# A decoder trunk on one core: norm and router as one stage, the shared expert moved ahead of the routed pairs

## The chip, the cores and the metric

The kernel runs on one core of one Trainium2 chip. The metric is the device time of one execution in microseconds (us), lower is better. All data is float32.

## What is computed

The input is a sequence of 272 tokens (16 learned meta tokens and 256 given ones) of width 1024. Two residual layers follow. Layer 0 mixes tokens with a gated linear recurrence and a gated delta rule side by side, layer 1 with a state space model and a gated output projection. Each mixer, and each mixture of experts (MoE) behind it, is closed by a LayerNorm over the sum of the scaled input and the result. Cut to the lines that the change touches:

```python
for layer in range(DEPTH):                       # DEPTH = 2
    mix = _ab_mixer(h, ...) if layer % 2 == 0 else _s5_mixer(h, ...)
    h = _layer_norm(ALPHA * h + mix, ln_mix_g[layer], ln_mix_b[layer])
    ffn = _moe_ffn(h, ...)
    h = _layer_norm(ALPHA * h + ffn, ln_ffn_g[layer], ln_ffn_b[layer])

def _moe_ffn(h, ...):
    scores = sigmoid(h @ w_router)                # 64 experts
    biased = scores + router_bias
    # 8 groups of 8 experts; a group's score is the sum of its two best; 4 groups stay
    # the 8 best biased experts of those groups are chosen; their scores, made to sum to 2.5, are the gates
    routed = sum over chosen e of gate_e * (silu(h @ w_gate[e]) * (h @ w_up[e])) @ w_down[e]   # 1024 -> 256 -> 1024
    shared = (silu(h @ sh_gate) * (h @ sh_up)) @ sh_down
    return routed + shared
```

Layer 1 computes its MoE for the 256 given tokens only (W = 256, two token tiles); layer 0 for all 272 (W = 272, three token tiles, the last of 16 tokens).

## The kernel before, in words

The activations `hT` lie in SBUF with the channels on the 128 partitions: 8 channel tiles (DC = 8) of W tokens each. Every stage is a block of its own with one hand-written program per engine: PE (matmuls), ACT (activations, copies), DVE (elementwise), POOL and SP (which issues most DMAs). The order of the work on an engine is the order in which it is written, and semaphores order the engines against each other. At the end of a block all engines meet before the next block begins.

For each layer the stages around the change are these.

- **The end of the mixer.** In layer 0 `group_mixers` projects to 8 output tiles; PE's L703 does the matmuls of a tile, DVE's L1035 adds it to `hT`. In layer 1 the gated projection (L2270 on PE, L2283 on ACT, L2289 and L2291 on DVE) does the same.
- **`layer_norm` (L1111 on).** PE sums over channels by multiplying with a matrix of ones (L1145, 8 matmuls), DVE makes the mean (L1174) and subtracts it from each tile (L1177), ACT squares each (L1160), PE sums the squares (L1149), ACT takes the root (L1162), DVE the reciprocal (L1179), DVE multiplies each tile (L1182), ACT applies gain and shift (L1166). For layer 0 SP issues, at the start of this stage, the router's weights and tables (L1089 to L1092), the shared expert's weights (L1095, L1097) and the weights of the first two pairs of experts (L1076, L1082). The norm behind the MoE (`source="acc"`) first adds `acc` to `hT` on DVE (L1172); the last one is the last stage but the writing out. In layer 0 that norm's block also carries SP's loads for the next mixer (L2059 to L2071).
- **`router_and_shared` (L1187 on).** PE makes the logits with `hT` as the stationary operand and the router's weights moving (L1228, 3 x 8 matmuls of 64 columns in layer 0), turns the normed tokens into rows (L1237), which ACT copies (L1275) and SP stores to DRAM (L1221), and multiplies with the shared expert's gate weights (L1243, 16 matmuls; ACT applies SiLU, L1278). DVE chooses the experts in a chain of small operations (L1293 to L1325), each of which waits for the one before. PE then makes the rank of each token within its expert (L1249) and turns mask and gates (L1255); DVE writes `places_gates` and the largest count (L1327 to L1336).
- **`experts` (L1339 on).** The 64 experts go in 32 pairs, 64 slots each. At the start three pairs are prepared one behind the other: DVE makes a selection (L1588), PE spreads the pair's row of places and gates (L1438, L1439), ACT copies the gates (L1549), DVE makes the scatter matrix and the token indices (L1602, L1606, L1611), POOL gathers the tokens' rows (L1411). Then, per pair: gate and up projection (L1461), turning the next pair's tokens (L1447), turning the activation (L1482), the combine of the pair before into 8 tiles (L1474 on PE, L1629 on DVE into `acc`), the spreading for the pair three ahead, the down projection (L1494). ACT's SiLU (L1562) comes right behind the gate and up projection. SP loads the weights of pair q+2 into the place of pair q as its matmuls end. Behind pair 0 comes the shared expert's up projection (L1522, 16 matmuls) with DVE's product (L1658); behind each of pairs 1 to 4 come two of the 8 tiles of its down projection (L1531) and DVE's `hT = ALPHA * hT + ...` (L1664). Pairs 5 to 28 run in a hardware loop, four to an iteration, pairs 29 to 31 behind it.

## Time and profile before

| quantity | value |
|---|---|
| median of 3 runs | 1783.89 us |
| lowest and highest run | 1783.6 and 1790.15 us |
| the profiled execution's own time | 1779.24 us |
| its span in the profile | 1777.5 us |
| PE, busy share of the span | 92% |
| DVE, ACT, POOL, busy share | 43%, 21%, 14% |
| mean granted clock of PE | 0.952 |
| DMA, mean over the span | 295 GB/s |

The profile is of one execution. Busy time of PE is the time in which it has matmuls under way; the granted clock is the share of full speed at which PE may run, so the same matmul is longer at a lower one. A float32 matmul shows as two records, so 16 records are 8 matmuls; a turning (a transpose) shows as one.

### The profile page before, as it was taken

The numbers are of one execution on the slowest core, as the hardware profiler recorded it, in microseconds if no ns is written. First come the engines' busy times: TensorE is split into PE (matmuls) and PEld (weight loads), VectorE is DVE, ScalarE is ACT, GpSimd is POOL, SyncE is SP. The second block draws the span as 40 slices with busy tenths as digits, with TensorE's granted clock in tenths as the row PEclk, the third lists the DMA queues.
The fourth block names the chain that finished last, engine by engine and source line by source line (L and its number), as shares of the span: only waits on it lengthen the run. The fifth ranks groups of instructions, "written<-read, shape, count | busy, mean of one in ns | idle before, by whom it ended". The sixth has DMA issues, their size and how long they took to land. (4 is left out here: it accounts for less than half of the span.)

```text
span 1777.5 us, 26595 instructions
## 1 busy us (share of the span) xinstructions
PE 1633.7 (92%) x9863; PEld 987.4 (56%) x9863; DVE 769.3 (43%) x1814; ACT 380.3 (21%) x798; POOL 249.7 (14%) x325
## 2 busy tenths in 40 slices
PE   7999889897799999999999877977999999999995
PEld 5787668775345444444444456863544444444444
DVE  3879567413234344334433455132434433443334
ACT  3765452203001111111111110130111111111112
POOL 5789243000000000000000000000000000000000
PEclk9999998798899999999999968988999999999998
DMA  7688260028588999999999270664999999999970
GB/s 259 209 164 260 84 182 3 1 95 314 233 344 340 409 421 425 423 417 421 421 420 421 100 301 3 242 248 190 362 369 413 425 424 425 427 424 425 424 322 25
DMA packets 101518, 524.87 MB, mean 295 GB/s; under 512 B 34020, under 2 KB 39012, under 8 KB 66620
## 3 DMA queue, kind: packets, MB, share of 16 engines
q1 hardware_dynamic: 90780, 480.62, 68.4%
q0 software_dynamic: 10656, 43.13, 6.3%
q8 instruction: 56, 0.92, 0.2%
q14 instruction: 26, 0.21, 0.0%
HBM read 510.80 MB, written 17.10 MB: 297 GB/s over the span
## 5 line engine op out<-in xcount | busy, mean ns | idle before, releaser
L1461 PE MATMUL e_b<-experts,e_xgT 128*64 128x512 f32 x2048 | 454.9, 597 | 8.1 <-DVE hT L1664 5.2
L1461 PEld LDWEIGHTS e_b<-experts,e_xgT 128*64 128x64 f32 x2048 | 150.3, 138 | 298.1 <-issue 292.5
L1474 PE MATMUL e_b<-e_sg,e_ys 128*128 128x272 f32 (+1 forms) x1024 | 239.0, 386 | 1.7 <-ACT e_ys L1572 1.7
L1494 PE MATMUL e_b<-experts,e_aT 128*64 128x512 f32 x1024 | 233.9, 598 | 3.7 <-DVE acc L1629 3.7
L1635 DVE TENSOR_TENSOR e_ac<-e_sl,e_b 128x256 f32<-128x256 f32 x64 | 27.0, 422 | 441.3 <-ACT e_sl L1562 441.3
L1629 DVE TENSOR_TENSOR acc<-acc,e_b 128x272 f32<-128x272 f32 (+1 forms) x512 | 200.4, 427 | 17.1 <-PE e_b L1474 10.8
L1474 PEld LDWEIGHTS e_b<-e_sg,e_ys 128*128 128x128 f32 x1024 | 188.3, 190 | 33.8 <-ACT e_ys L1572 3.4
L1411 POOL DMA_INDIRECT e_xg<-rows_dram,e_idx x64 | 60.1, 939 | 980.3 <-DVE e_idx L1611 972.0
L241 PE MATMUL proj<-hT,dense_ring 128*128 128x272 f32 x768 | 185.8, 401 | 10.2 <-DMA dense_ring<-in_w_in 10.2
L241 PEld LDWEIGHTS proj<-hT,dense_ring 128*128 128x128 f32 x768 | 148.1, 194 | 44.1 <-issue 13.4
L1494 PEld LDWEIGHTS e_b<-experts,e_aT 128*64 128x64 f32 x1024 | 70.7, 136 | 133.3 <-issue 116.7
L1562 ACT ACTIVATE e_sl<-e_b 128x256 f32<-128x256 f32 x64 | 24.6, 384 | 448.2 <-PE e_b L1461 448.2
L1645 DVE COPY e_ys<-e_b 128x512 f32<-128x512 f32 x64 | 44.3, 692 | 136.9 <-PE e_b L1494 136.9
L1447 PEld LDWEIGHTS e_b<-ident,e_xg 128*128 128x128 f32 x512 | 56.2, 144 | 54.8 <-issue 52.5
L1572 ACT COPY e_ys<-e_b 128x512 f32<-128x512 f32 x64 | 37.5, 585 | 229.3 <-PE e_b L1494 229.3
L1549 ACT COPY e_gsb<-e_b 128x272 f32<-128x272 f32 (+1 forms) x64 | 24.2, 379 | 236.4 <-PE e_b L1439 236.4
L1447 PE MATMUL e_b<-ident,e_xg 128*128 128x128 f32 x512 | 71.6, 284 | 3.0 <-DVE e_hit L1606 3.0
L703 PE MATMUL mix<-y,dense_ring 128*128 128x272 f32 x256 | 60.9, 398 | 1.4 <-DVE y L1024 1.1
L411 DVE SCALAR_TENSOR_TENSOR qkv<-cin,conv_w,qkv 128x272 f32<-128x272 f32 x48 | 41.7, 870 | 42.6 <-ACT qkv L299 41.7
L1438 PE MATMUL e_b<-places_gates,e_selw 64*128 64x272 f32 (+1 forms) x128 | 48.0, 456 | 12.8 <-DVE e_selw L1588 12.8
L2270 PE MATMUL glu<-acc,dense_ring 128*128 128x256 f32 x256 | 58.3, 392 | 1.3 <-PEq L106 1.3
L703 PEld LDWEIGHTS mix<-y,dense_ring 128*128 128x128 f32 x256 | 49.0, 193 | 11.9 <-DVE y L1024 1.3
(389 smaller groups left out, 1743.4 us busy)
## 6 DMA issues: line engine op xcount, KB each, us to landing
experts<-in_moe_gate_up SPq DMA_DIRECT2D x128, 2048.0 KB, 12.3
experts<-in_moe_down SPq DMA_DIRECT2D x128, 1024.0 KB, 10.6
dense_ring<-in_w_in SPq DMA_DIRECT2D x48, 512.0 KB, 4.5
dense_ring<-in_w_out SPq DMA_DIRECT2D x4, 2048.0 KB, 7.9
dense_ring<-in_s_w_out SPq DMA_DIRECT2D x4, 2048.0 KB, 12.8
s_cw_dram<-s_out POOLq DMA_DIRECT2D x4, 1024.0 KB, 5.4
s_cw<-s_cw_dram SPq DMA_DIRECT2D x4, 1024.0 KB, 12.0
s_wb<-s_wb_dram SPq DMA_DIRECT2D x2, 2048.0 KB, 19.1
```

What stands on the lines that cost most here:

```text
L241: mm = pe.matmul(ps[g % 4][:, 0:T], slot[:, n % SLOTS_IN, c, :], hT[:, c, :], start=(c == 0), stop=(c == DC - 1))
L411: step.done(dve.scalar_tensor_tensor(out=dst, in0=src[:, j:j + T], scalar=w(j), in1=dst, op0=ALU.mult, op1=ALU.add))
L703: mm = pe.matmul(out, ring[:, m // 4, c, (m % 4) * P:(m % 4 + 1) * P], y[:, q * DC + c, :], start=(c == 0), stop=(c == DC - 1))
L1411: pool.indirect_dma_start(out=xg[:, u % 2, :], out_offset=None, in_=mem["rows_dram"], in_offset=bass.IndirectOffsetOnAxis(ap=idx[:, u, :], ...
L1438: pe.matmul(t0b[:, 0:W], selw[0:E, u % 2, :], pg[0:E, 0:W], start=True, stop=True)
L1447: mm = pe.transpose((t0b, t1b)[c // 4][:, (c % 4) * P:(c % 4 + 1) * P], xg[:, u % 2, c * P:(c + 1) * P], ident[:])
L1461: mm = pe.matmul(gub[e * SLOTS:(e + 1) * SLOTS, :], xgT[:, u % 2, c, e * SLOTS:(e + 1) * SLOTS], gu_w(2 * (u % 2) + e)[:, c, :], start=(c ...
L1474: pe.matmul(cb[m % 4][:, 0:W], ys[:, m * P:(m + 1) * P], sg[:, u, :], start=True, stop=True).then_inc(cmm, 1)
L1494: mm = pe.matmul(yb[e * SLOTS:(e + 1) * SLOTS, :], aT[:, f, e * SLOTS:(e + 1) * SLOTS], dn_w(2 * (u % 2) + e)[:, f, h * BLOCK:(h + 1) * BL ...
L1629: dve.tensor_tensor(acc[:, m, 0:W], acc[:, m, 0:W], cb[m % 4][:, 0:W], ALU.add).then_inc(addd, 1)
L1645: dve.tensor_copy(ys[:, BLOCK:], y1b[:]).then_inc(ye1, 1)
L2270: mm = pe.matmul(ps[m % 4][:, 0:W], ring[:, b % 2, c, (m % 4) * P:(m % 4 + 1) * P], yT[:, c, :], start=(c == 0), stop=(c == DC - 1))
```

## The change

1. The column sums of the norm behind the mixer go into the mixer's last stage, each behind the projection two tiles later.
2. That norm and the router become one stage, `norm_and_route`. The logits are taken from the centred, not yet scaled tiles with the router's weights (multiplied by the norm's gain, on POOL) as the stationary operand: 8 matmuls of W columns; scale and shift are applied to the 64 x W result, and the scores are turned to tokens-on-partitions. Root and reciprocal become Ln and Exp. Group comparison and top-8 are joined over the token tiles. The shared expert's up projection and product now stand in this stage.
3. For layer 0 all these loads are issued in this stage: router, shared expert, pair 0, then the rows' stores, then pair 1. For layer 1 the router's loads move ahead into the mixer's last stage.
4. In `experts` the three first pairs are spread into three different pairs of PSUM banks one right behind the other, and all 8 tiles of the shared down projection, with `acc = ALPHA * hT + ...`, stand ahead of pair 0. `acc` is no longer set to zero, the loop holds pairs 1 to 28, and the norm behind the MoE reads `acc` directly, without the addition.
5. PSUM is one tensor for the whole kernel instead of one set per stage.

```diff
@@ group_mixers, PE: column sums joined
+                def column_sum(m):
+                    pe.wait_ge(added, DC + m + 1)
+                    pe.matmul(bank[4][:, 0:T], mem["ones"][:], hT[:, m, :], start=(m == 0), stop=(m == DC - 1))
+
                 for m in range(DC):
                     project(m, 1)
+                    if m >= 2:
+                        column_sum(m - 2)
+                column_sum(DC - 2)
+                column_sum(DC - 1)
...
@@ layer_norm (the one behind the MoE)
-                    if source == "acc":
-                        pe.wait_ge(added, c + 1)
-                    mm = pe.matmul(sums[:, 0:W], ones[:], hN[:, c, :], start=(c == 0), stop=(c == DC - 1))
+                    mm = pe.matmul(sums[:, 0:W], ones[:], acc[:, c, 0:W], start=(c == 0), stop=(c == DC - 1))
...
-                act.activation(rstd[:], sqs[:, 0:W], ACT.Sqrt, scale=1.0 / D, bias=eps[:, 2:3]).then_inc(rooted, 1)
+                act.activation(rstd[:], sqs[:, 0:W], ACT.Ln, scale=1.0 / D, bias=eps[:, 2:3]).then_inc(logged, 1)
+                act.wait_ge(logged, 1)
+                act.activation(rstd[:], rstd[:], ACT.Exp, scale=-0.5).then_inc(rooted, 1)
...
-                dve.reciprocal(rstd[:], rstd[:]).then_inc(inverted, 1)
-                dve.wait_ge(inverted, 1)
...
@@ norm_and_route, SP
+                if layer == 0:
+                    load_router(sp, k, mem, 0)
+                load_shared(sp, k, mem, layer)
+                if layer == 0:
+                    load_gate_up(sp, k, mem, 0, 0, 0)
+                    load_down(sp, k, mem, 0, 0, 0)
                 for tt, (t0, n) in enumerate(tiles):
                     sp.wait_ge(rows_c, 2 * tt + 2)
                     sp.dma_start(mem["rows_dram"][t0:t0 + n, :], rows[0:n, tt, :]).then_inc(stored, 16)
+                if layer == 0:
+                    load_gate_up(sp, k, mem, 0, 1, 1)
+                    load_down(sp, k, mem, 0, 1, 1)
...
@@ norm_and_route, PE, behind the sums of squares
+                for c in range(DC):
+                    mm = pe.matmul(bias_ps[0:E, 0:1], wr[:, c, :], shift(c), start=(c == 0), stop=(c == DC - 1))
+                mm.then_inc(biased, 1)
+                pe.wait_ge(weighed, 1)
+                for c in range(DC):
+                    mm = pe.matmul(lg_ps[0:E, 0:W], wg[:, c, :], hN[:, c, :], start=(c == 0), stop=(c == DC - 1))
+                mm.then_inc(logits, 1)
+
+                pe.wait_ge(scored, 1)
                 for tt, (t0, n) in enumerate(tiles):
...
+                    mm = pe.transpose(sc_ps[0:n, tt * E:(tt + 1) * E], lgT[:, t0:t0 + n], ident[0:E, 0:E])
+                mm.then_inc(score_turned, 1)
+
                 for i in range(2 * NT):
                     tt, half = i // 2, i % 2
                     t0, n = tiles[tt]
+                    pe.wait_ge(out, 4 * half + 4)
...
+                shared_half(0)
+                shared_half(1)
                 pe.wait_ge(selected, 1)
...
                 pe.wait_ge(gated, 1)
...
+                shared_half(2)
+                shared_half(3)
                 pe.wait_ge(counted, 1)
...
@@ experts, PE
-                turn(0, 0, (AHEAD, 16))
+                pe.wait_ge(mem["shared_down_ready"], 16 * (layer + 1))
+                for m in range(DC):
+                    if m >= 2:
+                        pe.wait_ge(sh_out, m - 1)
+                    for c in range(FC):
+                        mm = pe.matmul(cb[m % 2][:, 0:W], sh_down_w[:, c, m * P:(m + 1) * P], shared_act[:, c, :],
+                                       start=(c == 0), stop=(c == FC - 1))
+                    mm.then_inc(sh_dn, 1)
+                turn(0, 0, (1, 16))
+                pe.wait_ge(idf_ok, AHEAD)
                 pair(0, 0, 0)
...
-                with pe.Fori(0, (FULL - SHARED) // 4) as i:
+                pe.wait_ge(sh_out, DC)
+                with pe.Fori(0, FULL // 4) as i:
...
@@ experts, DVE
                 for q in range(AHEAD):
-                    select(q, q)
-                    places(q, q)
+                    select(q, q, start=True)
+                places(0, 0)
+                places(1, 1)
+                for m in range(4):
+                    residual(m)
+                places(2, 2)
+                for m in range(4, DC):
+                    residual(m)
                 turned_in(0, 0, True)
                 pair(0, 0, early=True)
...
```

`shared_half(0)` and `(1)` are the 16 gate matmuls (into banks 3 and 7), `(2)` and `(3)` the 16 up matmuls. The copies of the mask and of the gates for `places_gates` go from DVE to ACT, behind its two SiLUs.

## Rows read from the trace of the kernel before

**Rows 1.** Stretches: length, busy time (instructions) per engine, granted PE clock, DMA share, GB/s.

```profile
452.80:480.90 28.10, 20.65 (x82) 8.55 (x82) 7.87 (x29) 3.37 (x8) 3.86 (x4) 0.70 0.37 128
...
508.00:992.00 484.00, 480.00 (x2302) 229.13 (x2304) 186.64 (x488) 63.70 (x143) 25.30 (x27) 1.00 0.96 399
```

**Rows 2.** Timeline, SiLU of pairs 1, 5, 31 of layer 0, then of layer 1.

```profile
496.29 0.38 ACT L1562 ACTIVATE e_sl<-e_b 128x256 f32<-128x256 f32 x1 [14.69 <-PE e_b L1461]
...
572.77 0.38 ACT L1562 ACTIVATE e_sl<-e_b 128x256 f32<-128x256 f32 x1 [9.67 <-PE e_b L1461]
...
994.00 0.38 ACT L1562 ACTIVATE e_sl<-e_b 128x256 f32<-128x256 f32 x1 [6.28 <-PE e_b L1461]
...
1243.83 0.38 ACT L1562 ACTIVATE e_sl<-e_b 128x256 f32<-128x256 f32 x1 [14.23 <-PE e_b L1461]
...
1318.89 0.38 ACT L1562 ACTIVATE e_sl<-e_b 128x256 f32<-128x256 f32 x1 [9.53 <-PE e_b L1461]
...
1733.95 0.38 ACT L1562 ACTIVATE e_sl<-e_b 128x256 f32<-128x256 f32 x1 [6.28 <-PE e_b L1461]
```

**Rows 3.** Timeline: up projection behind pair 0 and start of pair 1, layers 0 and 1.

```profile
480.90 7.60 PE L1522 MATMUL e_b<-hT,dense_ring 128*128 128x272 f32 x32
...
489.08 7.09 PE L1461 MATMUL e_b<-experts,e_xgT 128*64 128x512 f32 x32 [0.57 <-issue]
...
1228.90 7.17 PE L1522 MATMUL e_b<-hT,dense_ring 128*128 128x256 f32 x32
```

**Rows 4.** Timeline of layer 0's norm, on PE, DVE and ACT.

```profile
407.70 3.90 PE L1145 MATMUL ln_sums<-hT,ones 128*128 128x272 f32 x16 [1.60 <-PEq L106]
...
413.07 3.93 PE L1149 MATMUL ln_sqs<-ln_sq,ones 128*128 128x272 f32 x16 [1.47 <-ACT ln_sq L1160]
...
419.45 2.91 DVE L1182 TENSOR_TENSOR hT<-hT,ln_rstd 128x272 f32<-128x272 f32 x8
419.93 4.14 ACT L1166 ACTIVATE hT<-hT,ln_par 128x272 f32<-128x272 f32 x8 [2.40 <-DVE hT L1182]
```

**Rows 5.** The last router table's loads: time to landing, both layers.

```profile
DMA to landing us min/median/max: 4.7/7.9/11.0
```

**Rows 6.** Timeline of layer 0's router stage.

```profile
425.55 8.88 PE L1228 MATMUL r_b<-router_w,hT 128*128 128x64 f32 x48 [8.54 <-PEq L2362]
...
435.51 5.46 ACT L1275 COPY r_rows<-r_b 128x512 f32<-128x512 f32 x6 [0.68 <-PE r_b L1237]
...
439.70 7.50 PE L1243 MATMUL r_b<-hT,dense_ring 128*128 128x272 f32 x32
...
443.40 0.36 DVE L1319 TENSOR_TENSOR r_sel_gates<-r_mr,r_mb 128x192 f32<-128x192 f32 x1
...
447.13 1.73 PE L1249 MATMUL r_b<-after,r_sel_gates 128*64 128x272 f32 x6
...
451.87 0.14 DVE L1336 CAST count<-r_row 1x1 int32<-1x1 f32 x1
```

**Rows 7.** Timeline, start of layer 0's experts: turning, gate and up, turning of pair 2.

```profile
462.64 1.94 PE L1447 MATMUL e_b<-ident,e_xg 128*128 128x128 f32 x8 [1.54 <-DVE e_hit L1606]
...
465.46 9.26 PE L1461 MATMUL e_b<-experts,e_xgT 128*64 128x512 f32 x32 [0.88 <-DVE e_xgT L1621]
...
496.10 1.09 PE L1447 MATMUL e_b<-ident,e_xg 128*128 128x128 f32 x8
```

**Rows 8.** Groups by line: the shared down projection over both layers.

```profile
L1531 PE MATMUL e_b<-shared_act,dense_ring 128*128 128x272 f32 (+1 forms) x64 | 16.4, 399 | 0.0
```

**Rows 9.** Timeline, norms behind the MoE: SP in layer 0, the rest in layer 1.

```profile
1024.90 8.91 SPq L2071 DMA_DIRECT2D s_turns<-s_table_dram  x1
...
1752.01 6.02 PE L1145 MATMUL ln_sums<-hT,ones 128*128 128x256 f32 x16 [4.49 <-DVE hT L1172]
...
1761.77 1.28 ACT L1162 ACT_TABLE_LOAD   x1
...
1763.72 1.75 DVE L1179 RECIPROCAL ln_rstd<-ln_rstd 128x256 f32<-128x256 f32 x1 [2.42 <-ACT ln_rstd L1162]
```

283 lines of the change are left out of this document (149 added, 134 removed).

## The prediction

> **What bounds the kernel now.** I read the stretches first. Over pairs 2 to 30 of layer 0 PE is busy 480.0 of 484.0 us at a granted clock of 1.00, and the DMA engines are busy 96% [rows 1]. So the pairs are bound by PE, with the transfers close behind. The timeline of the SiLU, which follows each pair's gate and up projection, gives the length of a pair: from pair 5 to pair 31 the 26 intervals take (994.00 - 572.77) / 26 = 16.20 us in layer 0 and (1733.95 - 1318.89) / 26 = 15.96 us in layer 1, but pairs 1 to 5, which carry the shared down projection, take 76.5 us and 75.1 us for four [rows 2]. The reader is to see that whatever PE does between pairs is added in full. Between pairs 0 and 1 stands the up projection, alone on PE [rows 3]. Then I read the two serial stages ahead of the pairs. The norm is a relay between PE, DVE and ACT [rows 4]. In the router stage PE is the long chain: logits, the turning of rows at the pace of ACT's copies, then the shared gate matmuls, and the ranks start right at their end (447.13) although DVE had its choice at 443.8 [rows 6]. The start of the experts is a third serial stretch: from 480.9 back to 452.8 the granted clock is 0.70, and the same matmuls are slow [rows 1, 7].
>
> **The change, part by part.**
>
> *Up projection (on the path today, taken out between pairs).* Layer 0: 489.08 - 480.90 = 8.2 us; layer 1: 7.17 us and the same 0.57 us of waiting, 7.7 us [rows 3]. It reappears in the router stage, counted there. Here: **-15.9 us**.
>
> *Down projection behind pairs 1 to 4.* These four intervals become ordinary ones: 76.5 - 4 x 16.2 = 11.7 us and 75.1 - 4 x 15.96 = 11.2 us [rows 2]. The matmuls are 16.4 / 2 = 8.2 us of a layer [rows 8], the rest was waiting for DVE, and perhaps the entry into the loop, which stays. **-22.9 us**, bounds -21 and -23.
>
> *The same down projection ahead of pair 0.* Before, the time from the end of the router stage (452.0) to the first turning is 10.6 us in layer 0 [rows 6, 7], almost all latency of three rounds between DVE, PE and ACT. After, the three selections and spreadings go in one run; with the meeting of the engines I put them at 3.7 us, an estimate (a third of the 10.6). Then 8.2 us of matmuls at full clock follow, two banks deep, so DVE's additions run beside them, but DVE also does the places of three pairs there and PE queues behind `sh_out`. 3.7 + 8.2 = 11.9 us: later by 1.3 us; for layer 1, whose old latency was shorter (256 columns), 1.7 us. The first gather is issued early in this stretch and is covered by it. **+3.0 us**, bounds 0 (all in the old shadow) and +6 (DVE's additions set the pace).
>
> *Clock of pair 0.* With PE at work through that stretch it should not fall to the low level of 1.2 GHz: gate and up 9.26 us becomes 7.09 us and a turning 1.94 us becomes 1.09 us, 3.0 us a layer [rows 3, 7]. **-6.0 us**, bounds 0 and -6.
>
> *Norm and router of layer 0.* The column sums (3.90 us) run at the end of the mixer instead [rows 4]; PE is full there, so they cost 3.9 us, of which only the meeting of the engines in front of them is won, and a small block for constants still stands between. I take the sums of squares to end where they did, at 417.0. All of SP's loads now start about 3.6 us later, since the stage does. The last of the four router loads took 4.7 us to land at least and 11.0 us at most [rows 5]; at that point the queue is empty as before, so I take 4.7: issued at 412.6, landed at 417.3. POOL's product of weights and gain, which no row shows, is a 128 x 512 elementwise operation: 1 to 3 us, I take 1.5. The 16 bias records of PE run beside it. The logits are 16 records of 272 columns, 3.9 us [as rows 4], in place of 48 in 8.88 us at half clock [rows 6]: they end at 423. DVE multiplies the 64 rows, then scales 8 tiles (2.91 us) to 426.8, while ACT takes the sigmoid and then gain and shift in 4.14 us [rows 4], to 428.6. DVE's choice thus starts some 8 us earlier than before, is shortened by about 1.3 us of joined operations, and ends well before PE can use it. PE turns rows at the pace of ACT's copies, 5.46 us from 428.6, and is free at 433.2. Gate matmuls 7.50 us to 440.7 (447.2 before) [rows 6]; ranks and turnings 2.3 us, 443.0; up projection 7.50 us, 450.5; DVE's last product and the count 0.9 us, 451.4 where it was 452.0. So the 7 us that the shorter norm and logits win are spent on the up projection: -0.6 us. Against that, PE is nearly idle from 423 to 428.5, and before, idleness of about this length brought the clock down at the start of the experts; I add 1.5 us for gate matmuls that begin slow. Layer 1 goes the same way with its router tables already there. Both: **+1.8 us**, bounds -3 and +9. ACT carries more (the copies for `placed`), but behind its SiLUs and hidden under the up projection; the second pair's loads go behind the rows' stores, and 6.3 MB at the 399 GB/s of rows 1 is 16 us, done before 452, so covered; without that cover they would delay pair 1 only, which starts 30 us later.
>
> *Norms behind the MoE.* In layer 0 the stage ends when SP has issued the next mixer's loads (1033.8), behind all of the norm's own work [rows 9]; these are issued from the stage's start, so the shorter norm gives nothing. In layer 1 PE needn't wait for DVE's first addition: 0.5 us. There the reciprocal of 1.75 us goes and an Exp of 0.47 us comes. Whether Ln and Exp need a table load between them no row shows; the bounds are 0 and 1.28 us, the load in rows 9. I take it as needed, since the load there falls between two functions too: 1.28 + 0.47 = 1.75, no gain. **-0.5 us**, bounds -1.8 and 0.
>
> The Trainium skill, ScalarE: Activation LUTs, section "Table sets: the hidden batching unit", speaks for the other end: ln and exp share a set and need one load. By it the last norm would give 1.3 us more; the trace before has no Ln to compare with.
>
> The sum is -15.9 - 22.9 + 3.0 - 6.0 + 1.8 - 0.5 = **-40.5 us**. The profiled execution took 1779.2 us itself (span 1777.5), 4.7 us below the median of the runs; it would become 1738.7 us, and the median of 1783.9 becomes 1743.4 us. I forecast 1743 us, 2.3% faster.
>
> **Rivals.**
>
> *The clock stays low.* If PE counts as idle both in the router stage and ahead of pair 0, the gate matmuls run at half clock throughout. The last norm shows column sums of 256 columns at 6.02 us, against 3.90 us for even 272 at full clock [rows 4, 9]: a factor of 1.6. That makes 7.5 us longer by 4.5 us, 3.0 us more than counted, and pair 0 keeps its 3.0 us: +12 us over two layers, 1755 us. For it speaks 0.70 in the stretch before [rows 1]; against it, that PE now has 8 us of dense work there. 18%.
>
> *Better hidden than I count.* Gate matmuls at full clock (-3), the down projection in the old shadow (-3), no second table load (-1.3): 1736 us. 13%.
>
> *Router loads late in layer 0.* If the last one takes 11.0 us to land [rows 5], logits and all behind them come 6.3 us later: 1749 us. The queue is empty then, which speaks against it. 6%. In this case the stage does not become shorter as it says, but the pairs still do.
>
> *The transfers become the bound (the other side).* A pair moves 2 x 3 x 1024 x 256 x 4 bytes = 6.29 MB of weights and 0.52 MB of gathered rows. At 16.2 us this asks for 421 GB/s, from pair 0 on and without the slack of pairs 0 to 4. The mean over pairs 2 to 30 is 399 GB/s at a share of 0.96 [rows 1]. It decides as soon as less than 421 GB/s is granted: at 399 GB/s a pair takes 17.1 us, and 62 of them 0.9 us each, 56 us more: 1743 + 56 = 1799 us, slower by 0.8%. At 399 / 0.96 = 416 GB/s it is 16.4 us and +12 us, 1755 us. Against it: 26 intervals in a row at 16.20 us already draw these 421 GB/s without one wait of PE for experts' weights. 3% for the first, 3% for the second.
>
> Another 2% goes to a loss I do not see that eats nearly all.
>
> **How the numbers follow.** Forecast 55%, and the cases at 1736, 1755, 1749, 1755 us with 13, 18, 6 and 3%: faster by over 0.5% (8.9 us, about what a measurement of this kernel can tell from no change) is 95%. Within 0.5% is 2%, slower 3%. The range: the gain's terms are sure to a few us, the stage terms carry bounds of about +10 and -8; with the rival at 1755 inside, and 4 us for the scatter of medians, 1729 to 1760 us.
>
> **What would show it.** In the profile after: no matmul of the shared expert between pairs, SiLU intervals of 16.2 and 16.0 us from pair 1 on; from the end of the router stage to the first turning 12 us; gate and up of pair 0 in 7.1 us; the router stage of layer 0 ending 44 to 46 us after the mixer's last projection would have ended before; logits in 16 records right behind the bias records. Wrong would be: PE waiting for experts' weights inside the pairs (the rival of the transfers), a turning of rows or gate matmuls beginning later than 434 - 406 = 28 us after the mixer's last old projection, or pair 0 at 9 us.

## The result and the profile after

| | before | after |
|---|---|---|
| median of 4 runs each | 1783.74 us | 1737.51 us |
| lowest and highest | 1778.57 and 1790.15 us | 1735.66 and 1741.03 us |
| the profiled execution's own time | 1779.24 us | 1735.66 us |
| its span | 1777.5 us | 1733.6 us |
| mean granted clock of PE | 0.952 | 0.967 |

The ratio is 0.9741, with a 95% interval of 0.9705 to 0.9778: 2.6% faster, 46 us between the medians and 43.9 us between the profiled spans. The forecast was 2.3%, 1743 us, in a range of 1729 to 1760 us.

The reader should start where the forecast's large terms are, in the pairs. The timeline of the SiLU after the change (start us, length us, engine, line, operation), pairs 0, 1, 5 and 31 of layer 0, then of layer 1:

```profile
473.56 0.38 ACT L1625 ACTIVATE e_sl<-banks 128x256 f32<-128x256 f32 x1 [7.39 <-PE banks L1534]
486.78 0.38 ACT L1625 ACTIVATE e_sl<-banks 128x256 f32<-128x256 f32 x1 [6.37 <-PE banks L1534]
551.61 0.38 ACT L1625 ACTIVATE e_sl<-banks 128x256 f32<-128x256 f32 x1 [6.36 <-PE banks L1534]
972.75 0.38 ACT L1625 ACTIVATE e_sl<-banks 128x256 f32<-128x256 f32 x1 [6.28 <-PE banks L1534]
...
1199.27 0.38 ACT L1625 ACTIVATE e_sl<-banks 128x256 f32<-128x256 f32 x1 [7.38 <-PE banks L1534]
1212.45 0.38 ACT L1625 ACTIVATE e_sl<-banks 128x256 f32<-128x256 f32 x1 [6.36 <-PE banks L1534]
1276.32 0.38 ACT L1625 ACTIVATE e_sl<-banks 128x256 f32<-128x256 f32 x1 [6.36 <-PE banks L1534]
1691.24 0.38 ACT L1625 ACTIVATE e_sl<-banks 128x256 f32<-128x256 f32 x1 [6.28 <-PE banks L1534]
```

Against [rows 2], layer 0 first: pair 1 to pair 5 takes 64.83 us where it took 76.48, and 63.87 us where it took 75.06. Pair 5 to pair 31 takes 421.14 and 414.92 us, against 421.23 and 415.06: the steady pairs did not change. Pair 0 to pair 1 is 13.2 us in both layers (21.5 and 21.1 before). All that is gained in the pairs is gained in the first five.

Then the stretch ahead of them. The timeline of the changed kernel from the end of the mixer to pair 0 of layer 0, PE's main rows, with the count that closes the router stage, and the same for layer 1:

```profile
409.45 1.54 PE L752 MATMUL banks<-hT,ones 128*128 128x272 f32 x6
414.23 3.93 PE L1255 MATMUL banks<-r_sq,ones 128*128 128x272 f32 x16 [3.25 <-ACT r_sq L1314]
418.31 1.09 PE L1259 MATMUL banks<-ln_par,router_w 128*64 128x1 f32 x16
419.43 3.88 PE L1263 MATMUL banks<-hT,r_wg 128*64 128x272 f32 x16
...
433.95 8.75 PE L1290 MATMUL banks<-hT,dense_ring 128*128 128x272 f32 x32
442.63 1.73 PE L1298 MATMUL banks<-after,r_sel_gates 128*64 128x272 f32 x6
444.82 7.60 PE L1290 MATMUL banks<-hT,dense_ring 128*128 128x272 f32 x32
453.12 0.14 DVE L1407 CAST count<-r_row 1x1 int32<-1x1 f32 x1
456.48 8.19 PE L1592 MATMUL banks<-shared_act,dense_ring 128*128 128x272 f32 x32
464.51 1.04 PE L1520 MATMUL banks<-ident,e_xg 128*128 128x128 f32 x8
466.43 7.09 PE L1534 MATMUL banks<-experts,e_xgT 128*64 128x512 f32 x32 [0.88 <-DVE e_xgT L1681]
...
1141.08 6.35 PE L1255 MATMUL banks<-r_sq,ones 128*128 128x256 f32 x16 [2.69 <-ACT r_sq L1314]
...
1160.24 8.69 PE L1290 MATMUL banks<-hT,dense_ring 128*128 128x256 f32 x32
1181.77 8.62 PE L1592 MATMUL banks<-shared_act,dense_ring 128*128 128x256 f32 x32
...
1192.14 7.09 PE L1534 MATMUL banks<-experts,e_xgT 128*64 128x512 f32 x32 [0.88 <-DVE e_xgT L1681]
```

The count comes at 453.12 instead of 451.87 [rows 6], the first turning at 464.51 instead of 462.64, and yet gate and up of pair 0 take 7.09 us and not 9.26, the turning 1.04 and not 1.94 [rows 7]. The stretches that answer to [rows 1], the first of them begun 2.9 us behind the count and not 0.9 us, are these (length; busy time of PE, PEld, DVE, ACT, POOL; granted clock, DMA share, GB/s):

```profile
456.00:480.00 24.00, 22.49 (x110) 12.25 (x110) 9.78 (x31) 3.16 (x8) 3.87 (x4) 1.00 0.52 185
500.00:980.00 480.00, 476.71 (x2296) 227.17 (x2292) 187.31 (x490) 64.38 (x145) 25.30 (x27) 1.00 0.96 403
```

The clock ahead of and in pair 0 is 1.00, where it was 0.70; begun 0.8 us behind the count, at 453.90 us, the stretch is at 1.00 too. In layer 1 it is not quite so, 0.94 from 1178.5 to 1207 us, and the down projection takes 8.62 us there for its 256 columns. In the pairs nothing is new but their start.

For each stretch, between rows of the two timelines (plus is longer after):

| stretch | layer 0 forecast | layer 0 measured | layer 1 forecast | layer 1 measured |
|---|---|---|---|---|
| to the count of the router stage | +0.9 | +1.25, of it 1.2 ahead of the change | +0.9 | +1.2 for the stage, see below |
| count to first turning | +1.3 | +0.62 | +1.7 | +2.36 |
| first turning to SiLU of pair 0 | -3.0 | -3.06 | -3.0 | -2.58 |
| pair 0 to pair 1 | -8.2 | -8.32 | -7.7 | -7.87 |
| pairs 1 to 5 | -11.7 | -11.65 | -11.2 | -11.19 |
| pairs 5 to 31 | 0 | -0.1 | 0 | -0.1 |
| last SiLU to the state space stage, or to the end | 0 | +0.1 | -0.5 | -1.2 |
| state space stage and projection | | | 0 | -3.35 |

"Ahead of the change" is read from the mixer's own matmuls (L703 before, L702 after): a group of 16 records starts at 355.02 us before and at 356.24 us after, and of the change only the common PSUM tensor reaches what stands ahead of it. The moment scatters: in a second execution of each it is 356.40 and 352.05 us. In layer 1 the router stage is counted from the last sigmoid of the mixer's projection to the count: 40.36 us before, 41.57 us after. The measured terms add up to the 43.9 us of the spans. Most terms of the forecast hold to about 1 us. The last row of the table, 3.35 us in a stage to which the change adds only the column sums, is what it did not have, and it hides a miss beside it: the forecast's +0.9 us for the router of layer 1 includes these column sums, which make the mixer's projection 2.15 us longer (from the first to the last sigmoid 26.33 and not 24.18 us). Counted as the forecast counts, that term is +3.4 us, and the rest of the state space stage is 5.5 us shorter. That the totals agree so well, 43.9 and 40.5 us, is in part luck.

### The profile page after: what moved, and what is told of

Read it like the earlier page. It is cut to its first block and busy times, and to the rows that moved or that the text cites. A ratio compares the mean times of both kernels' runs of the same rounds, so it can differ in the third digit from the quotient of the medians.

```text
span 1733.6 us, 26681 instructions
## 1 busy us (share of the span) xinstructions
PE 1615.4 (93%) x9852; PEld 971.7 (56%) x9852; DVE 753.2 (43%) x1782; ACT 390.6 (23%) x810; POOL 247.8 (14%) x325
## 5 line engine op out<-in xcount | busy, mean ns | idle before, releaser
L1534 PE MATMUL banks<-experts,e_xgT 128*64 128x512 f32 x2048 | 450.5, 592 | 1.8 <-DVE e_xgT L1681 1.8
L1534 PEld LDWEIGHTS banks<-experts,e_xgT 128*64 128x64 f32 x2048 | 149.7, 137 | 290.7 <-issue 290.7
L1547 PE MATMUL banks<-e_sg,e_ys 128*128 128x272 f32 (+1 forms) x1024 | 238.8, 386 | 1.7 <-ACT e_ys L1635 1.7
L1567 PE MATMUL banks<-experts,e_aT 128*64 128x512 f32 x1024 | 233.8, 598 | 3.7 <-DVE acc L1689 3.7
L1689 DVE TENSOR_TENSOR acc<-acc,banks 128x272 f32<-128x272 f32 (+1 forms) x512 | 199.3, 425 | 18.2 <-PE banks L1547 11.9
L1547 PEld LDWEIGHTS banks<-e_sg,e_ys 128*128 128x128 f32 x1024 | 188.1, 190 | 33.9 <-ACT e_ys L1635 3.4
L240 PE MATMUL banks<-hT,dense_ring 128*128 128x272 f32 x768 | 184.6, 399 | 9.6 <-DMA dense_ring<-in_w_in 9.6
L240 PEld LDWEIGHTS banks<-hT,dense_ring 128*128 128x128 f32 x768 | 147.3, 193 | 43.4 <-issue 13.2
L1567 PEld LDWEIGHTS banks<-experts,e_aT 128*64 128x64 f32 x1024 | 69.0, 136 | 134.6 <-issue 115.3
L1520 PE MATMUL banks<-ident,e_xg 128*128 128x128 f32 x512 | 69.8, 279 | 0.0
L702 PE MATMUL banks<-y,dense_ring 128*128 128x272 f32 x256 | 61.3, 396 | 1.4 <-DVE y L1031 1.1
L702 PEld LDWEIGHTS banks<-y,dense_ring 128*128 128x128 f32 x256 | 48.7, 192 | 11.8 <-DVE y L1031 1.3
```

What stands on the lines that cost most here:

```text
L240: mm = pe.matmul(ps[g % 4][:, 0:T], slot[:, n % SLOTS_IN, c, :], hT[:, c, :], start=(c == 0), stop=(c == DC - 1))
L702: mm = pe.matmul(out, ring[:, m // 4, c, (m % 4) * P:(m % 4 + 1) * P], y[:, q * DC + c, :], start=(c == 0), stop=(c == DC - 1))
L1520: mm = pe.transpose((t0b, t1b)[c // 4][:, (c % 4) * P:(c % 4 + 1) * P], xg[:, u % 2, c * P:(c + 1) * P], ident[:])
L1534: mm = pe.matmul(gub[e * SLOTS:(e + 1) * SLOTS, :], xgT[:, u % 2, c, e * SLOTS:(e + 1) * SLOTS], gu_w(2 * (u % 2) + e)[:, c, :], start=(c ...
L1547: pe.matmul(cb[m % 4][:, 0:W], ys[:, m * P:(m + 1) * P], sg[:, u, :], start=True, stop=True).then_inc(cmm, 1)
L1567: mm = pe.matmul(yb[e * SLOTS:(e + 1) * SLOTS, :], aT[:, f, e * SLOTS:(e + 1) * SLOTS], dn_w(2 * (u % 2) + e)[:, f, h * BLOCK:(h + 1) * BL ...
```

## The experiments

Ten more kernels ran, and both kernels once more, in three jobs; the kernel before had medians of 1779.74, 1781.34 and 1780.24 us there. A stretch is always read from the profiled execution.

### Both kernels once more

> The kernel before once more, for its profile. In the changed kernel the state space mixer (from its first matmul to the last sigmoid of its output projection) took 122.7 us, of which 2.3 us are the new column sums, against 126.0 us before, though none of its work changed; the granted clock in its first 40 us was higher. Theory: the clock falls at another moment in each execution, so a second profile of the kernel before can show anything from 121 to 126 us there. Rival: the clock there depends on what the change does, and before shows 126.0 +- 0.5 us again. Everything else of before should repeat within 0.3 us per stage.

> The changed kernel once more, for its profile. By the theory of chance the state space mixer takes another time than 122.7 us by over 1 us; by the rival it repeats within 0.5 us. The router stage of layer 0 (end of the mixer's last addition to the count) repeats at 43.2 us, the first turning comes 11.3 us after the count, gate and up of pair 0 take 7.1 us.

No edit. The times were 1784.09 and 1728.69 us, spans 1782.3 and 1726.3 us. The pairs repeat to 0.05 us: 76.48, 421.25, 75.05 and 415.03 us before, 64.83, 421.12, 63.87 and 414.95 us after. Other stretches don't. The last addition of layer 0's mixer starts at 406.1 and 407.5 us in the two executions of before, at 409.6 and 405.5 us after; from the first matmul of the state space stage to the last sigmoid of the projection it is 126.04 and 129.09 us before, 122.69 and 122.66 us after; and the router stage of layer 1 is 41.57 us once and 38.49 us once, with the sums of squares at 6.35 us in the first. So the 7 us between the two executions of the changed kernel lie ahead of and between the parts that the forecast computed.

Several expectations failed here. The router stage of layer 0 takes 42.23 us in the second execution, not 43.2 or the first one's 43.47, and the first turning comes 12.60 us behind the count, not 11.3: the spreadings run at the low clock (granted 0.66 from 448 to 452 us, 0.66 us for a record that took 0.39), and the down projection starts 4.68 us behind the count and not 3.36. The two differences cancel: from the mixer's last addition to the SiLU of pair 0 it is 63.91 and 63.87 us. And the state space stage: by the theory of chance it should have taken another time by over 1 us; it repeated within 0.03 us, as the rival said, and the kernel with root and reciprocal below, which is the same up to there but for the norm behind the MoE of layer 0, has 122.65 us. The kernel before did not repeat (126.04 and 129.09 us), as the rival said it would. So neither theory came out whole.

### The up projection left out

> The changed kernel without the shared expert's up projection (32 records in the router stage of each layer) and with a multiplication by one in place of the product; it leaves out the factor h @ sh_up. Theory: in its new place the up projection is still on the path, because PE carries the whole stage, so each layer's router stage ends about 6.5 us earlier (the count needs only DVE's maximum and one turning behind the ranks): 13 us less than the changed kernel, ratio to it 0.9925. Rival: the stage hides it behind ACT and DVE: under 2 us in all.

```diff
-                shared_half(2)
-                shared_half(3)
...
-                    dve.wait_ge(sh_gu, FC + m + 1)
-                    dve.tensor_tensor(shared[:, m, 0:W], shared[:, m, 0:W], bank[(1, 2)[m]][:, 0:W],
-                                      ALU.mult).then_inc(sh_mul, 1)
+                    dve.tensor_scalar(shared[:, m, 0:W], shared[:, m, 0:W], 1.0, None, ALU.mult).then_inc(sh_mul, 1)
```

The shared expert lacks its up projection and the product. 1726.98 us (1724.08 to 1730.04), ratio 0.9696 (0.9661 to 0.973); against 0.9741 that is 8 us less, where 13 were expected, and the intervals overlap; the one run of the changed kernel in this job took 1728.69 us, so the stretches tell more than the total. The router stage ends 35.98 us after the mixer's last addition, 7.5 us sooner than the 43.47 of the changed kernel (6.3 us sooner than its second execution), and in layer 1 at 35.83 instead of 41.57, 5.7 us sooner. So the up projection sets the length of the stage in its new place. But in layer 0 most of that time came back ahead of pair 0. PE in the profile of this kernel, behind the shared down projection:

```profile
442.18 7.93 PE L1588 MATMUL banks<-shared_act,dense_ring 128*128 128x272 f32 x32
452.28 1.97 PE L1516 MATMUL banks<-ident,e_xg 128*128 128x128 f32 x8 [2.17 <-DMA e_xg<-rows_dram,e_idx]
455.13 9.05 PE L1530 MATMUL banks<-experts,e_xgT 128*64 128x512 f32 x32 [0.88 <-DVE e_xgT L1677]
```

The first gather is now late (2.17 us of waiting), the clock goes down in that pause, and pair 0 is slow again. The first turning comes 14.71 us behind the count, not 11.39 (12.60 in the second execution), and the SiLU 11.94 us behind that, not 9.05. From the mixer's last addition to the SiLU of pair 0 it is 62.63 us without the up projection and 63.91 us with it: of the 7.5 us only 1.3 are left. In layer 1, with the gather in time, nothing comes back. A stage that gets shorter runs into the gather. In layer 0 the queue is full of weights at that time: the busy share of the DMA engines is 0.97 from 450 to 458 us after the change, and here 0.99 until 452 us. The first gather is issued 41.4 us behind the mixer's last addition here, 44.4 and 44.5 us in fill_route and fill_both, 45.8 us in the interleaved kernel, 47.7 and 48.4 us in the two executions of the changed one, and it takes 9.2, 7.5, 7.7, 6.5, 4.9 and 4.7 us to land: issued over 7 us, it lands within 2.5 us, at 50.6 to 53.1 us in all six. That the loads of the first two pairs set this moment I read from these rows; no run moved the loads.

### The down projection left out

> The changed kernel without the shared expert's down projection ahead of pair 0; acc starts as ALPHA * h alone, so the shared expert is left out of the result. Theory: its 8.2 us per layer stand in time in which PE waited anyway and keep PE's clock up: without it the first turning comes 1.5 to 2.5 us earlier per layer, but the matmuls of pair 0 run at the low level and take 3 us longer: within 3 us of the changed kernel in all. Rival: it is on the path: 8 us less per layer, 16 us in all.

```diff
-                for m in range(DC):
-                    if m >= 2:
-                        pe.wait_ge(sh_out, m - 1)
-                    for c in range(FC):
-                        mm = pe.matmul(cb[m % 2][:, 0:W], sh_down_w[:, c, m * P:(m + 1) * P], shared_act[:, c, :],
-                                       start=(c == 0), stop=(c == FC - 1))
-                    mm.then_inc(sh_dn, 1)
...
-                    dve.wait_ge(sh_dn, m + 1)
-                    dve.scalar_tensor_tensor(out=acc[:, m, 0:W], in0=hN[:, m, :], scalar=ALPHA,
-                                             in1=cb[m % 2][:, 0:W], op0=ALU.mult, op1=ALU.add).then_inc(sh_out, 1)
+                    dve.tensor_scalar(acc[:, m, 0:W], hN[:, m, :], ALPHA, None, ALU.mult).then_inc(sh_out, 1)
```

The result lacks the shared expert. 1736.9 us (1733.32 to 1743.58), ratio 0.9748 (0.9713 to 0.9783): no faster than with it, as expected. PE, ahead of pair 0 of layer 0:

```profile
464.59 1.94 PE L1520 MATMUL banks<-ident,e_xg 128*128 128x128 f32 x8 [5.80 <-DMA e_xg<-rows_dram,e_idx]
467.40 9.09 PE L1534 MATMUL banks<-experts,e_xgT 128*64 128x512 f32 x32 [0.88 <-DVE e_xgT L1674]
```

The first turning comes 9.65 us behind the count (11.39 with the projection, 12.60 in the second execution) and 9.67 us in layer 1 (12.32 and 12.27). So 16 matmuls of 8.2 us cost 1.7 to 3.0 us there, the rest lies in the shadow of the first gather, for which PE waits 5.80 us without them. And pair 0 at the low clock takes 2.9 and 2.8 us more. Taken together the projection is free in its new place: from the count to the SiLU of pair 0 it is 21.59 and 21.50 us without it, 20.44 and 21.36 us with it in the first execution, 21.64 and 21.31 us in the second. This is the strongest single fact behind the result: 22.8 us go from pairs 1 to 5, and nothing comes back.

### The column sums back in the norm

> The changed kernel with the column sums of the norm ahead of the router back at the start of the norm stage, in both layers. Theory: joined to the mixer they save only the meeting of the engines, and in layer 1 they leave PE idle for 3 us ahead of the sums of squares, which then run at the low clock (6.35 us against 3.72 us before); undone, layer 1's sums of squares take 3.7 us again and the whole is within 1.5 us of the changed kernel, perhaps faster. Rival: joining saves its full 3.9 us per layer, so undone the kernel is 7 to 8 us slower.

```diff
                     project(m, 1)
-                    if m >= 2:
-                        column_sum(m - 2)
-                column_sum(DC - 2)
-                column_sum(DC - 1)
...
+                for c in range(DC):
+                    mm = pe.matmul(sums[:, 0:W], ones[:], hN[:, c, :], start=(c == 0), stop=(c == DC - 1))
+                mm.then_inc(summed, 1)
```

Layer 1 likewise, and DVE waits for the sums. 1738.0 us (1732.84 to 1745.59), ratio 0.9771 (0.974 to 0.9803); against 0.9741 for the change whole the intervals overlap, and the difference of 5 us is unclear. In the profile the sums take 5.59 us, at a low clock, after a pause of 2.27 us, at the start of the norm:

```profile
405.22 5.59 PE L1250 MATMUL banks<-hT,ones 128*128 128x272 f32 x16 [2.27 <-PEq L2426]
```

From the mixer's last addition to the count of layer 0 it is 47.32 us, 3.85 us more than after (5.1 more than in the second execution), and the mixer is about 2.3 us shorter: joining them is worth some 1.5 to 2.8 us in layer 0. In layer 1 the router stage takes the same 41.55 us. The sums of squares there are back at 3.72 us, as expected, but the second execution of the changed kernel has 3.72 us as well, so joining doesn't always slow them.

### The old kernel with PE kept at work ahead of pair 0

> The kernel before with 3 matmuls whose result nobody reads behind each of the three spreadings ahead of pair 0, in time in which PE waits for ACT and DVE. Theory: pair 0 is slow there because PE was idle, not because of its operands: gate and up of pair 0 takes 7.1 us instead of 9.26 and 8.77 us, the first turning 1.1 instead of 1.9 us, so 4 to 6 us less over both layers. Rival: the clock has another cause: pair 0 stays at 9.3 us and the whole is unchanged or up to 2 us slower.

```diff
                     broadcast(q, q, first=True)
+                    for c in range(3):
+                        pe.matmul(cb[q % 2][:, 0:W], mem["ones"][:], hN[:, c, :], start=True, stop=True)
```

1772.71 us (1766.73 to 1777.14), ratio 0.9947 (0.9923 to 0.997). Nine matmuls in each layer whose result nobody reads make the old kernel 0.5% faster, and pair 0 is as quick as in the changed one:

```profile
454.27 3.09 PE L1518 MATMUL e_b<-hT,ones 128*128 128x272 f32 x6
...
462.76 1.06 PE L1447 MATMUL e_b<-ident,e_xg 128*128 128x128 f32 x8
464.70 7.09 PE L1461 MATMUL e_b<-experts,e_xgT 128*64 128x512 f32 x32 [0.88 <-DVE e_xgT L1623]
```

From the count to the SiLU of pair 0 it is 2.5 us less in layer 0 and 1.65 us less in layer 1, 4.2 us of the 8.6 between the medians; where the other 4.4 us come from the profile doesn't show. The forecast's term for the clock is shown by this run apart from all the rest of the change: it is PE's own work ahead of pair 0 that sets it. The Trainium skill, TensorE: Matmul & The Clock Gate, section "HAM oscillation — how this bites in real kernels", describes pauses between bursts of matmuls as what lowers the clock; this run agrees: the pauses ahead of the old kernel's spreadings were 1.9 to 2.0 us long, and with matmuls in them pair 0 is at the high level.

### 1 MB more for each pair

> The changed kernel with 1.05 MB more loaded per pair, into memory that the pairs don't use. It measures the rival of the transfers. A pair asks for 6.82 MB in 16.16 us, 422 GB/s; with the extra 7.86 MB it would be 487 GB/s. Theory: the limit lies little above what is drawn now, 426 to 440 GB/s, so the pair becomes bound by transfers at 17.9 to 18.5 us, and PE waits for experts' weights. Rival: there is much room, and the pair stays at 16.2 us.

```diff
+                def more(q):
+                    sp.dma_start(mem["dense"][:, 0, 0:EXTRA, :], k["moe_gate_up"][layer, 0].rearrange(
+                        "p (a n) -> p a n", n=BLOCK)[:, 0:EXTRA]).then_inc(extra, 16)
...
+                    sp.wait_ge(extra, q * 16 - 16)
+                    more(q)
```

With EXTRA = 4 this is 128 x 4 x 512 x 4 bytes, 1.05 MB, never read. 1866.59 us. Pairs 5 to 31 take 480.22 and 480.15 us, 18.47 us a pair. The stretch from 500 to 980 us, in the columns of the stretches above:

```profile
500.00:980.00 480.00, 441.42 (x2058) 203.46 (x2054) 170.38 (x453) 58.96 (x133) 24.35 (x26) 0.98 1.01 424
```

The list of waits over the whole execution (us in total, times, the longest), PE's row for the gate and up projection:

```profile
PE banks L1544 <- DMA experts<-in_moe_gate_up: 85.5, 52, 2.7
```

6.81 + 1.05 = 7.86 MB in 18.47 us are 426 GB/s, and the share is full. The changed kernel asks for 421 in layer 0, and the list shows what it would meet: 52 waits of PE, 85.5 us. So the rival of the transfers was 1% away there, and its place right: PE does wait for experts' weights once they are the bound.

In layer 1 the changed kernel is nearer than that. Its pairs take 15.96 us and ask for 6.81 / 15.96 = 427 GB/s. Two stretches of its profile, in the same columns:

```profile
500.00:940.00 440.00, 439.50 (x2122) 207.26 (x2116) 172.79 (x459) 59.97 (x135) 25.30 (x27) 1.00 1.01 423
...
1220.00:1680.00 460.00, 458.89 (x2246) 219.80 (x2242) 176.28 (x480) 63.30 (x143) 26.22 (x28) 1.00 1.01 425
```

The share is full in both, and PE has no wait for weights in either. But the gate and up weights take 14.7 us from issue to landing (median) between 1215 and 1275 us, 15.9 us between 1400 and 1460, and 17.0 us between 1600 and 1660, while in layer 0 it goes from 14.0 down to 11.6 us; with the extra load it is 24.9 us. So in layer 1 the queue falls behind slowly, and the loads, issued two pairs ahead, hide it until the layer ends. The Trainium skill, DMA: Bandwidth & Descriptors, section "Bandwidth", has 425 GB/s for 16 MB moved by one core; the runs agree.

### Gate matmuls between the turnings of the rows

> The changed kernel with the 16 gate matmuls of the shared expert set between the turnings of the rows, where PE waits for ACT's copies. Theory: PE's row of work bounds the stage, so what the gate matmuls take in these gaps comes off it: the ranks start 3 to 5 us earlier per layer, 6 to 10 us less in all. Rival: ACT's copies or DVE's choice of experts (ready at 433.6, the ranks at 442.6) become the bound at once, or the turnings come late behind the matmuls: under 2 us.

```diff
                     mm.then_inc(rows_t, 1)
+                    if i == 0:
+                        pe.wait_ge(gu_ready, 32 * (layer + 1))
+                        gate_part(4)
+                    elif i < 2 * NT - 1:
+                        gate_part(2)
+                gate_part(len(todo))
...
-                shared_half(0)
-                shared_half(1)
```

`gate_part(n)` issues the next n of the 16 gate matmuls. 1731.33 us (1729.42 to 1736.79), ratio 0.9726 (0.9703 to 0.975), where 6 to 10 us less than the changed kernel were expected. The ranks start 30.33 us behind the mixer's last addition, not 32.98 (31.74 in the second execution), and the router stages take 40.82 and 37.52 us instead of 43.47 and 41.57 (or 42.23 and 38.49 in the second execution of the changed kernel). That is 1 to 4 us a layer, by which execution of the changed kernel one compares with, and in layer 0 only 1.3 us of it reach the SiLU of pair 0 (62.63 us behind the mixer's last addition, as without the up projection); the ratios' intervals overlap, so the gain of the whole is unclear.

### PE's pauses filled

> The changed kernel with seven matmuls of ones by ones (128 columns each, about 1.6 us, result never read) ahead of each wait for the states in the state space stage of layer 1, where PE otherwise stands for 1.3 to 2.2 us per channel tile. Theory (PE's own pauses bring the granted clock down there, and the stage differs from one execution to the next by this alone: 121.7 to 130.9 us up to the last sigmoid in the executions so far): the stage's matmuls are all at the fast level (8 x 4 inputs in 2.25 us, not 2.9 to 3.7), the stretch takes 121.5 us or less, and the median is 2 to 5 us below the changed kernel's 1728 to 1737, with a narrower scatter. Rival (the clock falls by something that PE's work does not set, or DVE's chain sets the pace alone): stretch 122 to 130 us as before, median within 2 us of 1732; if the fill delays the far outputs, up to 4 us slower.

```diff
                     def far_outputs(a):
+                        for _ in range(7):
+                            pe.matmul(mem["bank"][7][:, 0:P], mem["ones"][:], mem["ones"][:], start=True, stop=True)
                         pe.wait_ge(stated, 2 * (a + 1))
```

1727.85 us (1726.4 to 1730.84), ratio 0.9705 (0.9674 to 0.9736). Two channel tiles of the state space stage after the change, one low and one high, and then the same place in this kernel:

```profile
1046.56 3.04 PE L2215 MATMUL banks<-hT,s_wb 32*128 32x68 f32 x64
...
1053.14 1.93 PE L2234 MATMUL banks<-s_state,s_cw 128*32 128x64 f32 x64 [1.26 <-DVE s_state L2293]
1055.01 3.70 PE L2215 MATMUL banks<-hT,s_wb 32*128 32x68 f32 x64
...
1063.32 2.23 PE L2215 MATMUL banks<-hT,s_wb 32*128 32x68 f32 x64
...
1069.12 1.11 PE L2234 MATMUL banks<-s_state,s_cw 128*32 128x64 f32 x64 [2.23 <-DVE s_state L2293]
```

```profile
1047.87 2.24 PE L2215 MATMUL banks<-hT,s_wb 32*128 32x68 f32 x64
1050.04 1.42 PE L2225 MATMUL banks<-hT,s_near_sb 32*32 32x256 f32 x32
1051.38 1.83 PE L2230 MATMUL banks<-ones 128*128 128x128 f32 x14
1053.68 1.11 PE L2236 MATMUL banks<-s_state,s_cw 128*32 128x64 f32 x64 [0.47 <-DVE s_state L2295]
```

At the high clock a tile takes 6.9 us with or without the fill (far outputs at 1024.90, 1031.76 and 1038.59 us after the change, at 1046.83 and 1053.68 us here), since DVE's chain sets it; at the low one 9.14 us, as in the interleaved kernel, whose far outputs start at 1018.66, 1027.80 and 1036.94 us. The twelve profiled executions without the fill have each between one and five of the eight far outputs at the low clock (1.93 us and not 1.11); the two with it have none. From the first matmul of the stage to the last sigmoid it is 117.58 us, less than in any other (121.1 to 130.9), and the six times lie within 4.4 us, where those of the other kernels with four or six runs lie within 5.4 to 12.8; fill_both, with the same fill, is at 8.6, so that the scatter gets narrower is not shown. Nor is the gain on the changed kernel certain: the ratio is 6.4 us below 0.9741 but the intervals overlap, and the one run of the kernel with root and reciprocal in the same job took 1728.15 us.

> The interleaved version (gate matmuls of the shared expert between the turnings of the rows) with such matmuls also in PE's pauses of the norm and router stage (10 ahead of the squares, 4 ahead of the scores, 5 ahead of the first rows) and 9 ahead of the first spreading of the experts; results never read. Theory: sums of squares 3.9 us in layer 1 as well (5.4 to 6.4 where the clock was low), ranks no later than in the interleaved version, down projection ahead of pair 0 in 8.2 us and not 9.2, so the first turning 1 us earlier in each layer; together 2 to 4 us less than the interleaved version's 1731.3, about 1728. Rival: the pauses were harmless and the fill only delays what stands behind it: same or up to 2 us slower.

```diff
+                fill(10)
                 for c in range(DC):
                     pe.wait_ge(squared, c + 1)
...
+                fill(4)
                 pe.wait_ge(scored, 1)
...
                 mm.then_inc(score_turned, 1)
+                fill(5)
...
+                for _ in range(9):
+                    pe.matmul(cb[0][:, 0:P], mem["ones"][:], mem["ones"][:], start=True, stop=True)
                 for q in range(AHEAD):
                     broadcast(q, q, first=True)
```

`fill(n)` issues n matmuls of ones of 128 columns. 1730.29 us (1726.94 to 1735.6), ratio 0.9724 (0.9691 to 0.9757): the same as the interleaved version on which it is built, where 2 to 4 us less were expected. The stages themselves got shorter, 37.82 and 36.04 us against 40.82 and 37.52, but in layer 0 the first turning comes 14.06 us behind the count (12.77), and the SiLU 10.79 us behind it (9.04). The profile of the next kernel, where the same is seen, has both reasons:

```profile
445.30 2.25 PE L1607 MATMUL banks<-ones 128*128 128x128 f32 x18 [1.66 <-PEq L106]
...
458.49 1.09 PE L1541 MATMUL banks<-ident,e_xg 128*128 128x128 f32 x8 [1.14 <-DMA e_xg<-rows_dram,e_idx]
460.47 8.78 PE L1555 MATMUL banks<-experts,e_xgT 128*64 128x512 f32 x32 [0.88 <-DVE e_xgT L1704]
```

The nine matmuls end at 447.5 us, 3.3 us behind the count, where the interleaved kernel begins the spreading 1.7 us behind its own: they delay the first gather, PE then waits for it, and the clock goes down for part of pair 0 (granted 0.66 from 460 to 465 us).

> Both of the preceding together. Theory: the gains add, 1724 to 1728 us. Rival: within 2 us of 1731.

1723.84 us (1717.13 to 1725.69), ratio 0.9674 (0.9642 to 0.9706), the fastest of all. Its interval ends where that of the changed kernel begins (0.9705). The ratios differ by 0.0067, 12 us. Of this 6.5 us lie between this kernel and fill_route (1730.29 and 1723.84), whose only difference is the fill in the state space stage; they ran in one job, and each of the six times of this kernel lies below each of the six of fill_route. The same fill alone on the changed kernel gives 0.9705 against 0.9741, 6.4 us. The rest, interleaving included, is within the uncertainty. Fewer matmuls ahead of the spreading were not tried.

### Root and reciprocal back in the norm behind the MoE

> The changed kernel with root and reciprocal put back in the norm behind the MoE alone (Sqrt on ACT, reciprocal on DVE). Theory (Ln and Exp need a table load each, 1.28 us, so that the second load and the Exp cost what the reciprocal did): in the last norm the time from the end of the sums of squares to the first scaled tile is within 0.3 us of the changed kernel's, with one table load fewer and the reciprocal of 1.75 us in its place. Rival (the load between Ln and Exp is hidden or cheaper than it looks): that stretch is 0.7 to 1.3 us longer here. The time of the whole can't tell.

```diff
-                act.activation(rstd[:], sqs[:, 0:W], ACT.Ln, scale=1.0 / D, bias=eps[:, 2:3]).then_inc(logged, 1)
-                act.wait_ge(logged, 1)
-                act.activation(rstd[:], rstd[:], ACT.Exp, scale=-0.5).then_inc(rooted, 1)
+                act.activation(rstd[:], sqs[:, 0:W], ACT.Sqrt, scale=1.0 / D, bias=eps[:, 2:3]).then_inc(rooted, 1)
...
+                dve.reciprocal(rstd[:], rstd[:]).then_inc(logged, 1)
+                dve.wait_ge(logged, 1)
```

1728.15 us in one run. The last norm after the change, and in this kernel:

```profile
1715.21 3.72 PE L1155 MATMUL banks<-ln_sq,ones 128*128 128x256 f32 x16 [1.42 <-ACT ln_sq L1166]
1717.52 1.28 ACT L1168 ACT_TABLE_LOAD   x1
1718.97 0.47 ACT L1168 ACTIVATE ln_rstd<-banks,eps 128x256 f32<-128x256 f32 x1 [0.16 <-PE banks L1155]
1719.46 1.28 ACT L1170 ACT_TABLE_LOAD   x1
1720.75 0.42 ACT L1170 ACTIVATE ln_rstd<-ln_rstd 128x256 f32<-128x256 f32 x1
1721.20 2.77 DVE L1185 TENSOR_TENSOR hT<-hT,ln_rstd 128x256 f32<-128x256 f32 x8 [4.15 <-ACT ln_rstd L1170]
```

```profile
1707.57 3.72 PE L1155 MATMUL banks<-ln_sq,ones 128*128 128x256 f32 x16 [1.42 <-ACT ln_sq L1166]
...
1711.84 1.75 DVE L1182 RECIPROCAL ln_rstd<-ln_rstd 128x256 f32<-128x256 f32 x1 [2.42 <-ACT ln_rstd L1168]
1713.62 2.77 DVE L1185 TENSOR_TENSOR hT<-hT,ln_rstd 128x256 f32<-128x256 f32 x8
```

From the end of the sums of squares to DVE's scaling it is 1721.20 - 1718.93 = 2.27 us with Ln and Exp and 1713.62 - 1711.29 = 2.33 us with root and reciprocal. The first table load lies under the matmuls, the second does not, and it costs what the reciprocal did.

## Why the prediction was right

*Up projection out from between the pairs*, -15.9 us: -8.32 and -7.87, -16.2 us. Right, as is that the router stage grows by it: leaving it out there made the stage 7.5 and 5.7 us shorter. But in layer 0 only 1.3 of the 7.5 us reach pair 0, so it costs less on the whole path than the stage shows. That "the 7 us that the shorter norm and logits win are spent on the up projection" held to 1 us: in layer 0 the gate matmuls began at 433.95 us, which is 433.2 plus the drift of 1.2 us less half a microsecond, and the count came at 453.12 against 451.4 + 1.5 + 1.2 = 454.1. The chain of sums that gave these moments (router weights, logits, scores, ACT's copies) was 1 us off at most. Two of its steps are loose: 5.46 us from 428.6 would be 434.1 and not 433.2, if PE had to wait for the last copy, and POOL's product, for which no row stood behind the 1.5 us, took 1.04 us.

*Down projection out from behind pairs 1 to 4*, -22.9 us: -22.8 us.

*The same ahead of pair 0*, +3.0 us: +0.62 and +2.36, 3.0 us. The sum is right here, the picture was incomplete; in the second execution it is +1.83 and +2.32, 4.2 us. I wrote that DVE's additions and the latency of the spreading set the pace; without the matmuls the first turning comes only 1.7 and 2.7 us sooner (2.95 and 2.6 against the second execution), since PE then waits 5.80 us for the first gather. I had called the gather "covered by" this stretch. It is, and it is also the floor under it: no_up, fill_route and fill_both all ran into it. The recorded text put the second pair's loads at "done before 452" and said that late ones "would delay pair 1 only". It counted 16 us for them alone, but they queue behind the shared expert's and pair 0's: issued from 435.62 us on, they took 16.6 us (gate and up) and 21.8 us (down) to land, the DMA share is 0.97 from 450 to 458 us, and what they meet is the first gather.

*Clock of pair 0*, -6.0 us: -3.06 and -2.58 us, 5.6 us, and the old kernel with unread matmuls shows the cause by itself. Layer 1 gave less because its gate and up projection had been at 8.77 us before, not at the 9.26 us that the forecast took for both.

*Norm and router*, +1.8 us: about 0 in layer 0 and +1.2 us in layer 1, 1.2 us; with the 2.15 us of column sums that layer 1's mixer now carries, which belong to this term, 3.4 us. In the second execution it is, counted in the same way, -1.2 us in layer 0 and +0.3 us in layer 1. The half-slow gate matmuls that I had added 1.5 us for are there: 8.75 us in layer 0 and 8.69 us in layer 1, where 7.5 and 7.1 are full speed. In layer 1 the sums of squares at 6.35 us are another slow stretch of this kind that I had not counted; the second execution of the same kernel has 3.72 us there, and gate matmuls at 7.50 us in layer 0 but 8.28 us in layer 1. This is the term where a forecast in tenths means nothing, because two executions of one program differ by 1 to 3 us.

*Norms behind the MoE*, -0.5 us: -1.2 us to the end, of it 0.6 us from column sums that ran at 5.38 and not 6.02 us. That Ln and Exp need two loads was taken and is so. The Trainium skill, ScalarE: Activation LUTs, section "Table sets: the hidden batching unit", says that one load serves ln and exp; the rows above show one ahead of each in this program, so its 1.3 us are not to be had as the loads stand.

*What was not in the sum*: the state space stage and projection of layer 1, 3.35 us shorter although it now carries 2.15 us of column sums. Nothing of the change touches its matmuls. Three of its tiles were at the low clock in the profile of before and one after; in other executions of the changed kernel's variants it was up to five. That such slow tiles come from PE's own pauses is shown (fill_s5). Whether the change makes them rarer is open. For it speaks that all three executions with the changed kernel's work up to there, the one with root and reciprocal in the norm included, have one slow tile and 122.65 to 122.69 us, and the three of the kernel before, the one with unread matmuls included, have three or four and 125.16 to 129.09 us. Against it: no_down, which is the changed kernel up to there but for the shared expert, has 127.11 us, no_up 130.93, and no_join, at 121.73 us and without the column sums there, has two slow tiles. The 3.35 us are as large as all that lies between the forecast's 40.5 us and the 43.9 us of the spans. The medians scatter too: the changed kernel's one later run, 1728.69 us, lies below all of its first four.

*The rivals.* "The clock stays low" happened in part (the gate matmuls, as counted), not to pair 0. "Better hidden" did not happen by any of its three means in the profiled execution; in the second one the gate matmuls of layer 0 did run at the full clock (7.50 us). Late router loads: the last landed 4.2 us after its issue at 414.08, the bias matmuls could start at 418.31, 1 us later than counted and not 6. The transfers cost nothing, but they were nearer than the forecast saw: 421 GB/s in layer 0 and 427 in layer 1 against a limit of about 426. Its figures of 399 and 416 GB/s for the limit rest on a misreading of [rows 1]: the stretch ends behind the last loads. From 508 to 960 us the kernel before moves 409 GB/s at a share of 0.99, from 960 to 992 us 257 GB/s at 0.61.

## What to carry to other kernels

Work that stands between dense groups of matmuls costs its full time, and the same work put into a stretch that waits for a latency chain can be free twice over: its own time lies in the shadow, and it keeps the clock up for what follows. Before placing it, find the floor of that stretch (here the first gather), because beyond it nothing is won, and shortening the stage ahead turns for the most part into waiting and a lower clock (6.2 of 7.5 us in layer 0). Where PE pauses for one or two microseconds again and again in a stage that another engine paces, a few matmuls that nobody reads are worth trying (here 6.5 us between two kernels that differ in nothing else), as long as they end before what they stand ahead of is ready.
